# The gate matrix of a routed layer: one-hots per group on VectorE and GpSimd, and one-hots per token on VectorE alone

## The reference, cut to what matters

```python
idx = i1 * PEER_N_KEYS + i2
g = jax.nn.softmax(best, axis=-1)
...
def chunk(args):
    ic, gc, xc = args
    act = jax.nn.gelu(jnp.einsum('ckd,cd->ck', u_tab[ic], xc), approximate=False)
    return jnp.einsum('ck,ckd->cd', (gc * act).astype(v_tab.dtype), v_tab[ic])
```

## Time and profile before

| | |
|---|---|
| timed runs, median | 2940.0 us (2939.86 to 2942.03) |
| profiled execution, span from first to last instruction | 2947.2 us |
| profiled execution, own time | none is given beside the span |
| instructions in the profile | 44691 |
| mean granted TensorE clock | 0.910 of full speed (2.4 GHz) |
| gate matrix stage, first layer | 388.55 to 519.71 us |
| gate matrix stage, second layer | 1638.6 to 1769.7 us |

### The profile page before, as it was taken

One profiled execution on the slowest core, in us unless ns is written; L12 is line 12 of the kernel. 1 busy time (PEld: TensorE's weight loads), 2 busy tenths in 40 slices (PEclk: granted clock), 3 DMA queues, 4 the chain that ended last, 5 costly groups with the idle time before them and its releaser, 6 DMA issues. The chain is left out here.

```text
span 2947.2 us, 44691 instructions
## 1 busy us (share of the span) xinstructions
PE 2511.8 (85%) x15512; PEld 2266.9 (77%) x15512; DVE 2067.6 (70%) x3346; ACT 1024.6 (35%) x1572; POOL 677.2 (23%) x548
## 2 busy tenths in 40 slices
PE   7859456999999999987593579999999999768898
PEld 7738346899999999877373468999999998758897
DVE  7585999666666666685769996666666665749652
ACT  4221122444444444342211224444444444444321
POOL 5571256000000000055712560000000000516340
PEclk9769778999999999987697789999999999889898
DMA  5424100555555555453241005555555554424201
GB/s 189 142 72 157 51 0 0 178 186 187 188 187 185 185 186 187 140 188 127 74 161 43 0 0 189 189 186 186 189 187 185 185 185 140 141 87 146 76 1 36
DMA packets 107647, 392.07 MB, mean 133 GB/s; under 512 B 11952, under 2 KB 13360, under 8 KB 107184
## 3 DMA queue, kind: packets, MB, share of 16 engines
q1 hardware_dynamic: 107568, 391.02, 39.4%
HBM read 389.93 MB, written 1.05 MB: 133 GB/s over the span
## 5 line engine op out<-in xcount | busy, mean ns | idle before, releaser
L570 PEld LDWEIGHTS bank<-x_parts,chunk_parts 128*128 128x128 f32 x6144 | 772.0, 192 | 23.1 <-DVE chunk_parts L1129 3.5
L570 PE MATMUL bank<-x_parts,chunk_parts 128*128 128x256 f32 x6144 | 778.5, 283 | 2.5 <-DVE chunk_parts L1129 2.5
L1129 DVE TENSOR_TENSOR chunk_parts<-weight_ring,chunk_parts 128x1024 fp32r<-128x1024 f32 x512 | 625.6, 1223 | 196.3 <-ACT chunk_parts L755 196.3
L582 PE MATMUL bank<-chunk_parts,weight_parts 128*128 128x512 f32 x3072 | 744.7, 391 | 0.6 <-DVE chunk_parts L1129 0.6
L755 ACT CAST chunk_parts<-weight_ring 128x1024 fp32r<-128x1024 f32 x512 | 535.7, 1047 | 359.3 <-PE bank L582 359.3
L582 PEld LDWEIGHTS bank<-chunk_parts,weight_parts 128*128 128x128 f32 x3072 | 560.7, 188 | 106.8 <-issue 0.9
L1121 DVE TENSOR_TENSOR work<-work,big 128x256 f32<-128x256 f32 x256 | 163.0, 637 | 278.7 <-ACT work L759 278.7
L1097 DVE TENSOR_TENSOR weight_ring<-constants,work 128x512 f32<-128x512 f32 x256 | 262.3, 1101 | 4.1 <-ACT work L741 4.1
L759 ACT ACTIVATE work<-bank 128x256 f32<-128x256 f32 x256 | 98.3, 384 | 466.8 <-PE bank L570 466.8
L547 PE MATMUL bank<-weight_ring 128*128 128x128 f32 x1024 | 184.1, 337 | 83.9 <-issue 74.8
L547 PEld LDWEIGHTS bank<-weight_ring 128*128 128x128 f32 x1024 | 160.8, 240 | 107.5 <-issue 98.9
(11 more groups left out here) (355 smaller groups left out, 2812.6 us busy)
## 6 DMA issues: line engine op xcount, KB each, us to landing
weight_ring<-in_experts SPq DMA_DIRECT2D x512, 512.0 KB, 3.3
big<-in_ada SPq DMA_DIRECT2D x48, 512.0 KB, 4.3
weight_ring<-in_w_in SPq DMA_DIRECT2D x40, 512.0 KB, 4.6
weight_ring<-in_wq SPq DMA_DIRECT2D x32, 512.0 KB, 3.2
weight_ring<-in_gdn_in SPq DMA_DIRECT2D x32, 512.0 KB, 3.3
weight_ring<-in_w_out SPq DMA_DIRECT2D x16, 640.0 KB, 4.0
weight_ring<-in_lru_in SPq DMA_DIRECT2D x16, 512.0 KB, 3.3
weight_ring<-in_w_kv SPq DMA_DIRECT2D x8, 512.0 KB, 4.4
```

Of the source, the lines that this page charges most:

```text
L570: last = nc.tensor.matmul(nc_ps[2 + n % 2][:, 0:T], a[:, j * P:(j + 1) * P], xr[:, x, j], start=(j == 0 and a is hi and x == 0), stop=(j = ...
L582: last = nc.tensor.matmul(nc_ps[4 + 2 * tt + c][:, 0:512], wr[:, x, n % 2, tt * P:(tt + 1) * P], v[:, c * 512:(c + 1) * 512], start=False, ...
L1129: nc.vector.tensor_tensor(split[:, k % SPLITS, 1], wring[:, (N_ALL + k) % WSLOTS, 0:D], split[:, k % SPLITS, 0].bitcast(F32), ALU.subtract ...
```

## The change

GpSimd's part is gone. VectorE makes the one-hots token by token. One scalar operation compares `iota` (128 columns) with one token's first key, read per partition from a column of `slot`, and multiplies the outcome with that token's gate, read the same way. A second compares with the second key. So a group takes 8 operations of 128x128 with one tensor input. Both rings have three tiles (`HOTS`), which is the same number of elements as before. One semaphore, `hots`, stands for both tiles of a group. All loops of the stage are written out as straight code.

```diff
+HOTS = 3
...
-    ha = hot(4, 4, P)
-    hb = hot(2, 4, P)
+    ha = hot(HOTS, 4, P)
+    hb = hot(HOTS, 4, P)
...
-                def gate_products(g, count):
-
-                    pe.wait_ge(s("first_gated"), count)
-                    pe.wait_ge(s("second_hot"), count)
-                    pe.wait_ge(s("g_kept"), count)
+                for g in range(GROUPS):
+                    pe.wait_ge(s("hots"), g + 1)
+                    if g == 0:
+                        pe.wait_ge(s("slots_kept"), 1)
+                    if g >= 2:
+                        pe.wait_ge(s("g_kept"), g - 1)
                     for j in range(4):
-                        last = nc.tensor.matmul(nc_ps[g % 2][:, j * P:(j + 1) * P], ha[:, g % 4, j], hb[:, g % 2, j], start=True, stop=True)
+                        last = nc.tensor.matmul(nc_ps[g % 2][:, j * P:(j + 1) * P], ha[:, g % HOTS, j], hb[:, g % HOTS, j], start=True, stop=True)
                     last.then_inc(s("g_ready"), 1)
...
-                with act.Fori(0, T // 8) as i:
-                    for g in range(2):
-                        act.wait_ge(s("g_ready"), i * 2 + (g + 5))
-                        nc.scalar.copy(G[:, bass.ds(i * 8 + 4 * g, 4)], nc_ps[g][:, :].rearrange("p (a c) -> p a c", a=4)).then_inc(s("g_kept"), 1)
+                for g in range(GROUPS):
+                    act.wait_ge(s("g_ready"), g + 1)
+                    nc.scalar.copy(G[:, 4 * g:4 * g + 4], nc_ps[g % 2][:, :].rearrange("p (a c) -> p a c", a=4)).then_inc(s("g_kept"), 1)
...
-                def gate_rows(g, position, count):
-                    pool.wait_ge(s("first_hot"), count)
-                    nc.gpsimd.tensor_tensor(ha[:, g % 4], ha[:, g % 4], slot[:, 2, bass.ds(position, 4)].unsqueeze(2).broadcast_to([P, 4, P]),
-                                            ALU.mult).then_inc(s("first_gated"), 1)
...
-                def one_hot(out, half, position, ready):
-
-                    nc.vector.tensor_tensor(out, iota.unsqueeze(1).broadcast_to([P, 4, P]),
-                                            slot[:, half, bass.ds(position, 4)].unsqueeze(2).broadcast_to([P, 4, P]),
-                                            ALU.is_equal).then_inc(s(ready), 1)
...
+                for g in range(GROUPS):
+                    if g >= HOTS:
+                        dve.wait_ge(s("g_ready"), g - HOTS + 1)
+                    for j in range(4):
+                        t = 4 * g + j
+                        nc.vector.tensor_scalar(ha[:, g % HOTS, j], iota, slot[:, 0, t:t + 1], slot[:, 2, t:t + 1], ALU.is_equal, ALU.mult)
+                        last = nc.vector.tensor_scalar(hb[:, g % HOTS, j], iota, slot[:, 1, t:t + 1], None, ALU.is_equal)
+                    last.then_inc(s("hots"), 1)
+                dve.wait_ge(s("g_kept"), GROUPS)
```

More of the change, by code:

```diff
@@ L219, in first_block @@
     hot.at = WSIZE + D
-    ha = hot(4, 4, P)
-    hb = hot(2, 4, P)
+    ha = hot(HOTS, 4, P)
+    hb = hot(HOTS, 4, P)
     GROUPS = T // 4
-    ROUND = 4
     out_e = big[:, 0:D]
@@ L328, in _ @@
                     if k == E_HOT:
-                        sp.wait_ge(s("g_ready"), 4 + GROUPS)
+                        sp.wait_ge(s("g_ready"), GROUPS)
                     sp.dma_start(wring[:, (N_ALL + k) % WSLOTS, 0:D], d_e[l, k]).then_inc(s(f"w_loaded{(N_ALL + k) % WSLOTS}"), 16)
@@ L538, in _ @@
                     last.then_inc(s("slots_turned"), 1)
-                def gate_products(g, count):
-                    pe.wait_ge(s("first_gated"), count)
-                    pe.wait_ge(s("second_hot"), count)
-                    pe.wait_ge(s("g_kept"), count)
+                for g in range(GROUPS):
[4 more added lines that the diff above has]
+                        pe.wait_ge(s("g_kept"), g - 1)
                     for j in range(4):
-                        last = nc.tensor.matmul(nc_ps[g % 2][:, j * P:(j + 1) * P], ha[:, g % 4, j], hb[:, g % 2, j], start=True, stop=True)
+                        last = nc.tensor.matmul(nc_ps[g % 2][:, j * P:(j + 1) * P], ha[:, g % HOTS, j], hb[:, g % HOTS, j], start=True, stop=True)
                     last.then_inc(s("g_ready"), 1)
[L550 to L555, removed]
+                pe.wait_ge(s("g_kept"), GROUPS)
                 pe.wait_ge(s("zeros"), 1)
@@ L742, in _ @@
                 last.then_inc(s("slots_kept"), 1)
-                act.wait_ge(s("slots_kept"), 1)
-                act.sem_inc(s("g_kept"), 2)
-                with act.Fori(0, T // 8) as i:
-                    for g in range(2):
-                        act.wait_ge(s("g_ready"), i * 2 + (g + 5))
-                        nc.scalar.copy(G[:, bass.ds(i * 8 + 4 * g, 4)], nc_ps[g][:, :].rearrange("p (a c) -> p a c", a=4)).then_inc(s("g_kept"), 1)
+                for g in range(GROUPS):
+                    act.wait_ge(s("g_ready"), g + 1)
+                    nc.scalar.copy(G[:, 4 * g:4 * g + 4], nc_ps[g % 2][:, :].rearrange("p (a c) -> p a c", a=4)).then_inc(s("g_kept"), 1)
                 def high(k, slot_, loaded, free):
@@ L836, in _ @@
                                             ALU.mult).then_inc(s("hit_keyed"), 1)
-                def gate_rows(g, position, count):
-                    pool.wait_ge(s("first_hot"), count)
-                    nc.gpsimd.tensor_tensor(ha[:, g % 4], ha[:, g % 4], slot[:, 2, bass.ds(position, 4)].unsqueeze(2).broadcast_to([P, 4, P]),
-                                            ALU.mult).then_inc(s("first_gated"), 1)
-                with pool.Fori(0, GROUPS // ROUND) as i:
-                    for g in range(ROUND):
-                        gate_rows(g, i * (4 * ROUND) + 4 * g, i * ROUND + (g + 1))
             @block.vector
```

## The result

The changed kernel takes 2911.7 us, the median of four runs (2911.05 to 2914.81), against 2939.9 us of the kernel before in the same session. The ratio is 0.9905 with a 95% interval of 0.9891 to 0.9919: 28 us faster (24 to 32). The forecast was 57 us. The sign was right, and so was what bounds the stage. The size was not: one term of the sum is wrong, because I misread a row.

A forecast was written before the change was run, and what follows sets the result against it. VectorE, stalled by GpSimd, was taken to bound the gate stage: 131.1 - 102.5 = 28.6 us saved per layer, 57.2 in two, off 2940.0 gives 2883 us; likeliest case 2876 to 2892, 8 in 10 within 2868 to 2912.

The forecast's parts named there:

- What bounds the stage: Gate-matrix stage before: VectorE sets the pace; GpSimd's multiply 1.31, held-back compare 0.54 and hand-over make 2.04 us a group.
- The price of the scalar compare: New 128x128 compares on VectorE: 0.200 us each, with or without the gate; 1.60 us a group, 102.4 us a stage.
- (c): Nearest price row, a 128x256 pair from SBUF taken as two-pointer: 0.265 us to the next, fixed part 0.133.
- What it adds on VectorE: Prediction's section pricing the 512 new scalar compares per layer from related trace rows, 102.4 us a stage.
- both bounds of the compare's price: Ends of the price per new compare, 0.193 and 0.207 us; a stage of 98.8 to 106.0, the kernel 2876 to 2890.
- The single pace: Rival: new compares miss the doubled pace, 0.264 us each, a stage 135.2 us, the kernel 2948 us; chance 0.09.
- The free pointer: Rival: pointer costs nothing between successive compares, 0.136 us each, TensorE sets 1.13 us a group, 2822 us; chance 0.03.
- the sixteen of the earlier trace: Price row: sixteen scalar subtracts of 128x128 from PSUM, 0.259 us each, fixed part 0.127.
- TensorE as the bound: Rival: granted clock stays 0.50 in the stage, 1.95 us a group, 2927 us, or 2905 with half so; chance 0.09.
- The cover: Slack before VectorE's wait for TensorE three groups earlier: 2.0 us, 1.15 at the low clock, so the wait costs nothing.
- Straight code: Rival: the stage's 512 straight-line compares starve an engine; gaps up to 9 us in all, widening the forecast's range to 2892.
- The rule on small tiles: Skill-page advice against the change: small tiles pay a fixed cost per instruction, so use at least 512 elements.

The follow-up runs named there:

- The useless multiplication: Kernel before in straight code, GpSimd's 64 multiplications per layer kept as idle work, TensorE waiting for the first one-hots, gates left out: 2943.0 us, ratio 0.9999.
- GpSimd's useless work: Changed kernel plus one GpSimd multiplication of 128x512 per group into tiles nobody reads, waited for only at the stage's end: 3027.0 us, ratio 1.0286.

## Why the prediction was right and wrong

**What bounds the stage: right.** The period of the kernel before is GpSimd's multiply and the compare that stood still beside it. The useless multiplication shows it: 2.05 us with nobody waiting for GpSimd inside the stage. In the Trainium skill, page "SBUF — State Buffer", section "Terms", VectorE and GpSimd arbitrate for a shared port pair, which one instruction holds exclusively. The trace agrees, for the operations with two tensor inputs and for the scalar compares; the loss per meeting was 0.84 to 0.86 us, less than GpSimd's recorded 1.15, 1.31 and 1.42. Part of each recorded duration lies beside a compare that had begun first and was not lengthened: 0.33 us in the earlier trace rows (397.02 to 397.35), 0.44 in the run with nobody waiting (421.58 to 422.02, where the next compare starts), 0.10 beside the changed kernel (429.82 to 429.92). What is left is nearly alike, 0.98, 0.98 and 1.05 us. That GpSimd itself stood still in that first part would fit this, but no run shows it.

**The price of the scalar compare: wrong by one term.** The step that failed is (c) in "What it adds on VectorE", and its consequence, that the fixed part is the same "with one and with two scalars", so that the gate's multiplication rides along at no cost: 0.200 us for a compare that took 0.257. I took the pair at 2667.94 in the earlier trace rows for operations with two pointers, tap and bias. The line has two callers: the recurrent layer passes a bias from SBUF, the delta rule layer passes none, so there the second scalar is the constant 0.0. The pair at 2667.94 belongs to the second. The summary by line (341/354/2465) mixes 8 of one kind with 24 of the other. By stretch of time, the eight with two pointers and the 24 with one stand in the trace of the kernel before like this, and below them a quiet pair with two:

```profile
L1380 DVE TENSOR_SCALAR big<-big,work x8: 402/411/2257, 2538.5 to 2561.1; 128x256 f32<-128x256 f32 x8
L1380 DVE TENSOR_SCALAR big<-big,work x24: 341/352/2465, 2667.9 to 2744.9; 128x256 f32<-128x256 f32 x24
...
2557.38 0.74 DVE L1380 TENSOR_SCALAR big<-big,work 128x256 f32<-128x256 f32 x2 [0.15 <-DVE big L1383]
```

The medians differ by 0.06 us, as those of the two new compares do (329 and 268 ns). 0.74 - 0.41 = 0.33 us from one to the next, a fixed part of 0.198 and not 0.133. With that row the compare with the gate costs 0.066 + 0.198 = 0.264, the other 0.066 + 0.133 = 0.199, a group 1.85 us, a stage 118.5, and the forecast would have been 2940 - 25 = 2915 us. Measured were 0.257 and 0.196. The wrong term is 4 x (0.257 - 0.200) x 128 groups = 29 us, and the other compare was 2 us too dear; the sum would have been 57 - 27 = 30, plus 1.2 from the gaps behind the stages, which the sum had left as they were. That 2911.7 us lies just inside the range of 2868 to 2912 is luck: the upper edge was widened for the rivals and not for this, and both bounds of the compare's price, 0.193 and 0.207, came from operations with one pointer.

**The single pace: fell.** With a fixed part of 0.127 or more the single pace would have shown 0.26 us from start to start where 0.196 stands. All of the new compares have 128 elements, so pace and fixed part are not measured apart; the doubled pace rests on the fixed part of the one-pointer rows, which gives 0.193 to 0.207.

**The free pointer: fell.** A compare with one costs about what the sixteen of the earlier trace rows gave (0.193 forecast from them, 0.196 measured), and not 0.136.

**TensorE as the bound: fell.** It waits 42.4 us for the compares in the first layer, and the granted clock went up to 1.00, as the forecast expected. The cover was as reckoned: VectorE waits for nothing, though the first groups run at the low clock (0.85 from 390 to 400 us).

**Straight code: right.** 512 compares in a row have no gap that shows (115.86 of 115.90 us busy), and the run with straight code alone gives a ratio of 0.9994.

**The rule on small tiles** that the prediction set against the change was not what bit. In the Trainium skill, page "VectorE: DVE Perf Modes", section "The TRN2 errata", the fixed cost is one per instruction. That the wide compare beats four narrow ones when GpSimd is idle agrees with it (0.60 against 0.78 us), but the larger term here is the second pointer, 4 x 0.06 = 0.24 us a group against 0.18.

## What to carry to other kernels

Before a row is used as the price of an operation, make sure which caller it comes from: one line of a helper can hold two forms whose names and shapes are the same, and a split by stretch of time separates them. On VectorE count the scalars that are read per partition: the second one cost 0.06 us per operation here, while a second arithmetic step was free. The first seems to cost as much (fixed part 0.07 for the cast, 0.13 with one scalar), but no run took it out. When VectorE is busy all of the time and GpSimd works beside it, compare the shortest and the longest duration of the same operation before calling the time work; moving three quarters of GpSimd's share to ScalarE, beside which no compare of a kind was stretched (681 to 689 ns for those of 128x512), gave more than moving all of it to VectorE.

## What was not expected of the hardware

With GpSimd's useless work beside the changed kernel, the granted clock was 0.50 (1.2 GHz) for the whole stage in both layers, although TensorE is shown busy for 78% of a stretch like this:

```profile
430.00:470.00 40.00, 31.12 (x121) 26.71 (x122) 40.00 (x121) 8.79 (x15) 17.22 (x16) 0.50 0.00 1
```

There TensorE's 2.07 us of matmuls at the low clock come every 2.67 us. In the changed kernel 1.16 us come every 1.81 and the clock is 1.00; in the kernel before 1.13 come every 2.05, and it goes to and fro. Since VectorE sets the pace in all three, the clock cost nothing in the stage. It shows in VectorE's gap behind the stage, when the last matmuls are waited for. Where the clock there was 0.50 to 0.51, the gap was 4.00 us (kernel before, first layer, 520 to 522 us) and 3.83 (beside the useless work, both layers); where it was 1.00, the gap was 2.99 (kernel before, second layer) and 2.88 (changed kernel, both layers). The prediction left the gap as it was; the 1.1 us of the first layer come from there.
